# The first mixer of a transformer kernel, written anew: latents by feature tiles, roots applied at evictions and in the exponential, unnormalised probabilities

## The reference, cut to what matters

```
mod = silu(c) @ ada_w[0] + ada_b[0]            # 6 x 1024: shift1, scale1, gate1, shift2, scale2, gate2
h = rms_norm(x, norm_mix) * (1 + scale1) + shift1
proj = h @ w_in                                # 672: q_lat 384, kv_lat 256, k_rope 32
q = rms_norm(q_lat, g_qa) @ w_qb               # 16 heads of 96 (64 + 32 rotated)
kv = rms_norm(kv_lat, g_kva) @ w_kvb           # 16 heads of 64 keys + 64 values
q = [q_nope, rope(q_rope)];  k = [k_nope, rope(k_rope) for every head]
q = rms_norm(q, g_q);  k = rms_norm(k, g_k)    # over the 96 of a head
o = softmax(q k^T * 96 ** -0.5) v
x = x + gate1 * (o @ w_o)
```

## Time and profile before

| | |
|---|---|
| Median of three runs | 2139.15 us (2138.95 to 2140.81) |
| The profiled execution's own time | 2137.76 us |
| Its span in the trace | 2136.0 us |
| PE, DVE, ACT, POOL busy | 93%, 68%, 52%, 15% of the span |
| First latents matmul | 48.5 us |
| Last latents matmul ends | 67.4 us |
| First scores of the attention | 132.4 us |
| First matmul of the output product | 188.3 us |
| First matmul of the first MLP | 220.9 us |

### The profile page before, as it was taken

How to read it: one execution, slowest core, us unless ns; L and a number is a source line. 1 busy time by engine, 2 the same in 40 slices (tenths; PEclk the granted TensorE clock), 3 DMA queues, 4 the chain that set the end, 5 groups by cost and what they waited for, 6 DMA issues and landing times.

```text
span 2136.0 us, 34628 instructions
## 1 busy us (share of the span) xinstructions
PE 1994.7 (93%) x14140; PEld 1845.9 (86%) x14140; DVE 1445.9 (68%) x2553; ACT 1114.7 (52%) x1831; POOL 323.8 (15%) x338
## 2 busy tenths in 40 slices
PE   2859899899999998999889989999999999999998
PEld 1747899899988888999788889999999998888886
DVE  6697785667677756654765556889997775555554
ACT  3545553422666645543555444446767764444444
POOL 3020000000000000000000000006886970000000
PEclk7879999999999999999999999999999999999999
DMA  7534688633534433565433434554444445555553
GB/s 272 185 123 153 206 259 268 201 120 130 197 129 158 140 118 120 187 188 177 168 129 109 149 128 149 178 183 163 150 149 161 143 140 182 187 189 187 188 189 120
DMA packets 97070, 356.24 MB, mean 167 GB/s; under 512 B 10688, under 2 KB 10816, under 8 KB 96528
## 3 DMA queue, kind: packets, MB, share of 16 engines
q1 hardware_dynamic: 83824, 305.04, 42.4%
q0 software_dynamic: 12656, 48.08, 7.1%
q10 hardware_dynamic: 432, 0.90, 0.1%
HBM read 352.93 MB, written 1.05 MB: 166 GB/s over the span
## 4 chain that ended last, share of the span: by engine, by line
PE 84%; DVE 10%; ACT 4%; DMA 1%; issue 1%; SPq 0%; DVEq 0%; POOL 0%; ACTq 0%
PE psum L523 23%; PE psum L525 23%; PE psum L524 23%; PE psum L516 14%; PE psum L530 2%; DVE wl L1637 1%; DVE araw L1620 1%; DMA first<-in_ada_w 1%; ACT wh L1119 1%; ACT sqh L1107 1%; ACT work L1107 0%; DVE first L1620 0%; DVE st L1627 0%; DVE C L1617 0%; DMA araw<-in_ada_w 0%
## 5 line engine op out<-in xcount | busy, mean ns | idle before, releaser
L1637 DVE TENSOR_TENSOR wl<-raw,wh 128x1024 fp32r<-128x1024 f32 (+1 forms) x564 | 689.7, 1226 | 446.3 <-ACT wh L1119 445.7
L1119 ACT ACTIVATE wh<-raw 128x1024 fp32r<-128x1024 f32 (+1 forms) x564 | 593.1, 1053 | 473.6 <-PE psum L525 446.3
L523 PE MATMUL psum<-peer_hh,wh 128*128 128x256 f32 x1152 | 332.0, 288 | 4.2 <-DVE peer_hl L1609 4.0
L525 PE MATMUL psum<-peer_hh,wl 128*128 128x256 f32 x1152 | 326.2, 283 | 0.0
L524 PE MATMUL psum<-peer_hl,wh 128*128 128x256 f32 x1152 | 324.8, 282 | 0.0
L523 PEld LDWEIGHTS psum<-peer_hh,wh 128*128 128x128 f32 x1152 | 218.1, 189 | 5.4 <-issue 4.4
L524 PEld LDWEIGHTS psum<-peer_hl,wh 128*128 128x128 f32 x1152 | 218.7, 190 | 0.0
L525 PEld LDWEIGHTS psum<-peer_hh,wl 128*128 128x128 f32 x1152 | 216.9, 188 | 0.0
L523 PE MATMUL psum<-wh,csh 128*128 128x512 f32 x512 | 202.9, 396 | 0.0
L525 PE MATMUL psum<-wh,csl 128*128 128x512 f32 x512 | 202.7, 396 | 0.0
L524 PE MATMUL psum<-wl,csh 128*128 128x512 f32 x512 | 202.7, 396 | 0.0
(11 more groups left out here) (436 smaller groups left out, 4778.8 us busy)
## 6 DMA issues: line engine op xcount, KB each, us to landing
raw<-in_mlp_w SPq DMA_DIRECT2D x128, 512.0 KB, 4.0
raw<-in_eu SPq DMA_DIRECT2D x128, 512.0 KB, 3.3
raw<-in_ev SPq DMA_DIRECT2D x128, 512.0 KB, 3.2
araw<-in_ada_w POOLq DMA_DIRECT2D x80, 512.0 KB, 4.8
raw<-in_dil_qk SPq DMA_DIRECT2D x48, 512.0 KB, 3.4
raw<-in_dil_v SPq DMA_DIRECT2D x24, 512.0 KB, 3.9
first<-in_ada_w SPq DMA_DIRECT2D x8, 1024.0 KB, 18.1
raw<-in_w_in SPq DMA_DIRECT2D x16, 512.0 KB, 3.3
```

The lines of the kernel that those rows point to most:

```text
L523: e.matmul(o, l[0], r[0], start=start, stop=False, skip_group_check=loose)
L525: i = e.matmul(o, l[1], r[0], start=False, stop=stop, skip_group_check=loose)
L1119: e.activation(b.wh[v % NSPLIT][:, 0:cols], b.raw[v % NRAW][:, 0:cols], ACT.Copy).then_inc(S.hi, 1)
L1637: e.tensor_tensor(b.wl[v % NSPLIT][:, 0:cols], b.raw[v % NRAW][:, 0:cols], b.wh[v % NSPLIT][:, 0:cols].bitcast(F32), ALU.subtract).then_in ...
```

## The change

Only the first mixer is written anew; the work of later stages stays, with two small shifts of modulation tiles.

- **Loads and modulation.** Eight blocks of scale and shift: blocks 0, 1, 3 and 5 (`PE_ADA`) come as plain weight columns and are projected on TensorE, with the column `silu(c)` (`ccol`, a stationary of one column) against 256 columns, eight float32 matmuls each; the row is evicted by ScalarE and turned into columns by two transposes. Blocks 2, 4, 6 and 7 stay multiply-and-sums on VectorE. SyncE's queue alternates the 16 loads of 512 KB with the units of `w_in`. GpSimd no longer computes. Four of the eight `gate1` tiles are likewise projected on TensorE, in four pieces that GpSimd loads (`mod`). The angles of the rotation are computed at the very start.
- **Latents.** `w_in` is now the stationary, in eight units, one for each feature block: each adds to five banks (feature tiles) and the rotated part of the keys at once, so block k needs only its own scale and shift. The latents come out feature-major; their halves are made without the root. The root of each latent is formed from a matmul of the squares with a column of ones, and multiplied at the eviction of keys, values and queries, as ScalarE's per-token scale.
- **Heads.** Keys and values first, then queries. Squares and sums are made unit by unit. Keys are scaled in four groups on VectorE; the root of a query head isn't applied to the query but as the scale of the exponential (`aq`). ScalarE evicts all transposes.
- **Attention.** Probabilities are turned unnormalised. The values product has the turned probabilities as stationary and 64 value columns moving, token-major output, divided by the sum for two heads at once, transposed (`oT`), and split. The steps are ordered scores(i), values(i-2), turning(i-1).
- **Output product.** In rows (`rows_unit`, used elsewhere before): unit c contracts over heads 2c and 2c+1 only and adds to four banks that hold all eight output blocks. The eight units stand between steps 12 and 19, one a step. The eight residual passes and the four squares come after the last one.
- **Order.** All of it is one list, `MLA_ORDER`, that every engine follows; it has 26 ticks in place of 35.

```diff
+PE_ADA = (0, 1, 3, 5)
+PE_MODS = 1
+def mla_order():
+    out = [("tick", 0), ("kv", 0), ("tick", 0), ("kv", 1), ("tick", 0), ("kv", 2), ("tick", 0), ("kv", 3),
+           ("kroot", 0), ("q", 0), ("kscale", 0), ("kscale", 1), ("mod", 0), ("q", 1), ("kT", 0), ("kscale", 2),
+           ("kT", 2), ("q", 2), ("kT", 4), ("kT", 6), ("kscale", 3), ("qsum", 0), ("q", 3), ("mod", 1), ("qrope", 0),
+           ("kT", 8), ("tick", 0), ("kT", 10), ("q", 4), ("qT", 0), ("kT", 12), ("tick", 0), ("q", 5), ("qT", 2),
+           ("kT", 14), ("qsum", 1), ("qT", 4), ("qroot", 0), ("qT", 6)]
+    out += [("mod", 2), ("mod", 3)]
+    outer = {12: 0, 13: 1, 14: 2, 15: 3, 16: 4, 17: 5, 18: 6, 19: 7}
+    for i in range(20):
+        if i in outer:
+            out.append(("hi", outer[i]))
+        out.append(("att", i))
+        if i == 1:
+            out += [("qrope", 1), ("modrow", 0)]
+        if i in (2, 3, 4, 5):
+            out += [("qT", 4 + 2 * i)]
+        if i == 3:
+            out.append(("modcol", 0))
+        if i in outer:
+            out.append(("lo", outer[i]))
+        if i in outer:
+            out.append(("wo", outer[i]))
+        if i in range(20):
+            out.append(("tick", 0))
...
 # TensorE
+        def ada(j):
+            ps = take("ada", j)
+            for k in range(8):
+                if k % 4 == 0:
+                    pe.wait_ge(S.early[2 * j + k // 4], 16)
+                mm(ps[0:1, 0:256], m.ccol[:, k:k + 1], first[:, j, k, :], k == 0, k == 7,
+                   mark=("ada done", j) if k == 7 else None)
+            give("ada", j, sem=S.act, key=("ada", "row", j))
+        def w_in(k):
+            if k == 0:
+                for c in (3, 4, 0, 1, 2):
+                    take("lat", c)
+            j = weights("mla_w_in", k)
+            pe.wait_ge(S.dve, at["n0", "lo", k])
+            h = sp(m.hh, k)
+            for c in (3, 4, 0, 1, 2):
+                o = b.psum[:, at["bank", "lat", c], 0:256]
+                w = wsp(j, c * 128, 128)
+                mm(o, w[0], h[0], k == 0, False, loose=True)
+                mm(o, w[0], h[1], False, False, loose=True)
+                mm(o, w[1], h[0], False, k == 7, loose=True, mark=("lat", c, "done") if k == 7 else None)
+            o, w = b.psum[0:32, at["bank", "lat", 2], 256:512], wsp(j, 640, 32)
...
+                give("kvb", s, t, sem=S.act, key=("kvb", "v", s, t))
+                if (s, t) == (0, 0):
+                    for c in (3, 4):
+                        give("lat", c, sem=S.act, key=("lat", "square", c))
+                    lat_sums("kv", (3, 4), 0)
+                if (s, t) == (0, 1):
+                    k_rope()
+                if (s, t) == (1, 0):
+                    lat_sums("q", (0, 1, 2), 1)
...
+        def s3(h):
+            c = h // 2
+            if h % 2 == 0:
+                take("mla", "o", c)
+            ps = b.psum[:, at["bank", "mla", "o", c], :]
+            pe.wait_ge(S.act, at["mla", "probT", h])
+            for t in range(2):
+                z = t * 128 + (h % 2) * 64
+                for kb in range(2):
+                    a = kb * 256 + t * 128
+                    mm(ps[:, z:z + 64], m.probT[:, h % 2, a:a + 128], m.kv[:, kb, h, 64:128], kb == 0, kb == 1,
+                       mark=("mla", "pv", h) if kb == 1 and t == 1 else None)
...
+        ada(0)
+        ada(1)
+        columns(0)
+        columns(1)
+        ada(3)
+        w_in(0)
+        columns(3)
+        for k in range(1, 8):
+            w_in(k)
+            if k == 1:
+                ada(5)
+            if k == 2:
+                columns(5)
...
+            elif kind == "att":
+                if i < 16:
+                    s1(i)
+                if 0 <= i - 2 < 16:
+                    s3(i - 2)
+                if 0 <= i - 1 < 16:
+                    s2(i - 1)
+                if i >= 4 and i % 2 == 0:
+                    s4((i - 4) // 2)
+            elif kind == "wo":
+                pe.wait_ge(S.dve, at["mla", "out", i])
+                rows_unit("mla_o", "mla_w_o", i, sp(m.hh, i), i == 0, i == 7)
+        for c2 in range(4):
+            square_sums("mla_o", c2, m.ring)
...
 # ScalarE
+        def step(i):
+            if 0 <= i - 1 < 16:
+                h = i - 1
+                ac.wait_ge(S.pe, at["mla", "turned", h])
...
+                act(m.probT[:, h % 2, :], bank("mla", "t", h), ACT.Copy, mark=("mla", "probT", h))
...
+                ac.wait_ge(S.dve, at["mla", "negmax", i])
+                for t in range(2):
+                    act(m.prob[:, i % 3, t * 256:t * 256 + 256], bank("mla", "s", i)[:, t * 256:t * 256 + 256], ACT.Exp,
+                        bias=m.st[:, 1, i, t:t + 1], scale=m.aq[0][:, t, i:i + 1], accum_out=m.st[:, 2, i, t:t + 1],
+                        mark=("mla", "exp", i))
...
 # VectorE
-MOD_GROUPS = [(16, 8), (24, 16), (40, 8), (48, 16), (64, 16), (80, 8), (88, 8)]
+MOD_GROUPS = [(16 + 4 * PE_MODS, 8 - 4 * PE_MODS), (24, 16), (40, 8), (48, 16), (64, 16), (80, 8), (88, 8)]
...
+        products(2)
+        rsqrt("n0", m.ntmp[:, 256:512], m.ntmp[:, 512:768], rs)
...
+        for j in range(8):
+            if j >= 3:
+                ada(j)
+            ahead(j - AHEAD)
+            low(j)
+            if j in (1, 3, 4):
+                products({1: 4, 3: 6, 4: 7}[j])
...
 # GpSimd
+        po.wait_ge(S.early[15], 16)
+        piece(0)
+        piece(1)
+        for kind, i in MLA_ORDER:
+            if kind == "mod":
+                po.wait_ge(S.pe, at["mod", i])
+                piece(i + 2)
+            elif kind == "tick":
+                tick(1)
+        mod_until(24)
...
 # SyncE
+    for j in (2, 0, 1):
+        early(2 * j)
+        early(2 * j + 1)
+    for j in range(3):
+        weights(j)
+    for j in range(3, 8):
+        early(2 * j)
+        early(2 * j + 1)
+        weights(j)
```

More of the change, by code:

```diff
@@ L733, in mla, with columns @@
-        for s in range(4):
+        first = m.first.rearrange("p (j k n) -> p j k n", j=8, k=8)
+        def ada(j):
[6 more added lines that the diff above has]
+            give("ada", j, sem=S.act, key=("ada", "row", j))
+        def columns(j):
+            ps = take("ada col", j)
+            pe.wait_ge(S.act, at["ada", "row", j])
+            for x in range(2):
+                z = PE_ADA.index(j) * 256 + x * 128
+                turn_row(ps[:, x:x + 1], m.row3[0:1, z:z + 128],
+                         ("ada", "col", j) if x else None)
+            give("ada col", j, sem=S.dve, key=("ada", "col out", j))
@@ new lines, in k_rope, with lat_sums @@
+        def k_rope():
+            ps = take("k rope")
+            pe.wait_ge(S.act, at["k rope in"])
+            for t in range(2):
+                x = e.transpose(ps[:, t * 32:t * 32 + 32], m.krT[0:32, t * 128:t * 128 + 128], ident[0:32, 0:32])
+            x.then_inc(S.pe, 1)
+            n[0] += 1
+            at["k rope turned"] = n[0]
+            give("k rope", sem=S.act, key="k rope out")
+        def lat_sums(key, tiles, z):
+            ps = take("lat sum", key)
+            pe.wait_ge(S.act, at["lat", "square", tiles[-1]])
+            for t in range(2):
+                for c in tiles:
+                    a = c * 256 + t * 128
+                    mm(ps[:, t:t + 1], m.sqL[:, a:a + 128], ones[:, 0:1], c == tiles[0], c == tiles[-1],
+                       mark=("lat", "sum", key) if t and c == tiles[-1] else None)
+            give("lat sum", key, sem=S.act, key=(("lat", key), "ms"))
@@ new lines, in kv, with q @@
+                if (s, t) == (1, 0):
+                    lat_sums("q", (0, 1, 2), 1)
+        def q(s):
+            ps = take("qb", s)
+            j = weights("mla_w_qb", s)
+            for t in range(2):
+                for k in range(3):
+                    pe.wait_ge(S.dve, at["lat", "lo", k])
+                    mm3(ps[:, t * 256:t * 256 + 256], sp(m.latT, k, 256, t * 128, 128), wsp(j, k * 256, 256),
+                        k == 0, k == 2, unit=t == 1 and k == 2)
+            give("qb", s, sem=S.act, key=("qb", "out", s))
+            if s == 0:
+                for c in range(3):
+                    give("lat", c, sem=S.act, key=("lat", "square", c))
@@ L1283, in mla @@
[L1283 to L1292 removed]
+                r = m.ls[:, 2, 2 + t:3 + t]
+                act(m.kv[:, t, 4 * s:4 * s + 4, :], p3, ACT.Copy, scale=r, mark=("kvb", "v", s, t))
@@ L1294, in mlp @@
+        for c2 in range(4):
+            square("mla_o", c2, m.ring, ("mla_o", "out", c2))
     def mlp(layer, norm, sums):
@@ L1937, in mla @@
[L1937 to L1946 removed]
+            ts(m.kk[:, s], m.ang, float(1 / (2 * np.pi)), 0.25 * s, ALU.mult, ALU.add)
+        own()
```

693 lines of the change are left out of this document (421 added, 272 removed).

## The result

The changed kernel takes 2092.85 us (median of 4 runs, 2090.2 to 2093.95) against 2139.05 us (4 runs, 2136.97 to 2140.81): a ratio of 0.9783, 95% interval 0.9766 to 0.98, 46.2 us less. The forecast was 2095 us in a range of 2084 to 2112. The profiled execution has a span of 2091.1 us and took 2092.84.

What follows compares the result with a forecast made beforehand. The prediction took TensorE to bound the kernel almost throughout. Terms -18.1 + 2.0 - 18.9 - 10.1 + 1.4 = -43.7 on 2137.8 us gave 2094, with 1.4 for the median 2095; range 2084 to 2112.

Steps and rivals of the forecast that it cites:

- What bounds the kernel: Whole kernel: TensorE has 84% of the chain of waits; only the stretch before the first MLP matmul, 220.9 us, changes.
- Start: Up to the first latents matmul: 48.5 us falls to 30.4, a gain of 18.1.
- Latents: The latents' product: 19.0 us grows to 21, a loss of 2.
- Latents to first scores: From the latents' end to the first scores: 64.9 us falls to 46, a gain of 18.9.
- Attention and output: Attention and output product: 81.6 us falls to 71.5, a gain of 10.1, with steps 2 to 11 at 2.85 each.
- Tail: From the output product to the first MLP matmul: 6.9 us grows to 8.3, a loss of 1.4.
- The rule against it: Query units: transposes don't engage the full clock and would pull it down; some 4 us at risk by the row.
- (a): Start and latents: one-column projections run at, or leave, the lower clock, 9.4 and about 3 us, 2107; chance 20%.
- (b): Attention: the old step of 3.5 us stays, ten steps by 0.65, 2102 us; chance 13%.
- (c): Latents to first scores: roots and scalings stay in front of TensorE, 64.9 us fall only to 57, 2106; chance 10%.
- (d): From 30.4 us to the MLP: no stall left, 5, 4 and 2 us go, 2084; chance 5%.
- (e): Through the mixer: the clock stays at its lower level, 2190 us, slower; chance 2%.

Runs made afterwards that it cites:

- experiment 5: Changed kernel with `vec` loaded before the row of the condition on ScalarE's queue: 2088.41 us, ratio 0.9765.
- experiment 10: Changed kernel with five GpSimd multiplications of 128 x 1024 put back at the start, on an unused buffer: 2094.32 us, ratio 0.9784.
- experiment 6: Changed kernel with all 16 scale and shift tiles issued before the weight units that wait for a split: 2089.59 us, ratio 0.9768.
- experiment 4: Changed kernel with query roots multiplied into the queries before turning, query transposes behind the modulation pieces: 2098.3 us, ratio 0.9813.
- experiment 9: Changed kernel with VectorE's 16 attention modulation tiles loaded only in their first 256 of 1024 columns: 2092.55 us, ratio 0.9776.
- experiment 1: Changed kernel with each head's probabilities normalised on VectorE before they are turned: 2111.49 us, ratio 0.9873.
- 11: Changed kernel with two extra VectorE multiplications a head on a tile nobody reads, without TensorE waiting: 2094.51 us, ratio 0.9783.
- 12: Changed kernel with TensorE's turning of a head waiting for VectorE's reciprocal, nothing multiplied there: 2096.69 us, ratio 0.9793.
- experiment 7: Changed kernel with the tail's table load moved in front of all four squares of the residual: 2090.55 us, ratio 0.9775.
- the three orders: Changed kernel with `vec` before the condition row, tiles before waiting weight units and table load before the squares, together: 2085.49 us, ratio 0.975.
- experiment 3: Changed kernel with all 16 scale and shift tiles on VectorE and none projected on TensorE: 2093.52 us, ratio 0.9794.
- experiments 2: Changed kernel with the eight output product units after the attention's last step, not between steps 12 and 19: 2102.55 us, ratio 0.9832.

## Why the prediction was right, point by point

**What bounds the kernel.** Right: everything outside the first mixer stayed within 1.2 us, and TensorE's chain share rose.

**Start.** The gain of 18.1 was 15.7. The term that was mis-sized is the beginning of the norm's sum: "near 12.6, the same constants land first, in another order" was 15.04, because the load of `vec` stands behind one of 512 KB on its queue; experiment 5 gives back 2.4 us of start. The projections' price of 3.4 us measured 3.5, the clock stayed at 1.00, the slowed VectorE passes shrank from 9.1 to 2.8 us. But experiment 10 shows that, with the blocks on TensorE, slow passes that end 2.6 us later delay the first latents matmul by only 0.63, and the keys by 1.3 through SyncE's queue; so these passes have slack, and part of the 6.3 us that they shed was hidden. What all of them slow would have cost was not run: in experiment 10 the two `na` passes were not.

**Latents.** The loss of 2.0 was 4.0. "Uncovered this is worth 3 us" was said of SyncE's queue and left out of the sum. It was uncovered: experiment 6 gains 3.8 us at the MLP, with 1.2 in the latents and 1.9 in the hole in front of the keys.

**Latents to first scores.** 44.7 for 46. TensorE's list was 41 and was busy 41.1. The first evictions of keys came 8.2 us behind the latents, not 6.5, past the 7 that I had named as a sign of a wrong step; it did no harm, since TensorE was gapless from 67 us on and the wait was only in front (3.1 us for the latents' low half and 0.6 at 63 to 67). That sign was badly chosen. The forecast has no lower clock there, and behind that wait it was 0.50 for some 3 us. That the queries' root chain is hidden was right. Its worth, 2.5 us by the forecast, was not measured by itself: the 5.15 of experiment 4 have the scalings and the later transposes in them.

**Attention and output.** 67.0 for 71.5. The step of 2.85 was 2.68, heads 12 to 15 took 21.1 for 22, the last four 15.2 for 15.5, and the 1.5 for a last low half cost 0.9 inside these 15.2. Three terms were mis-sized: the step (1.7 us in ten), heads 12 to 15 (0.9), and the last four with the low half (1.8). The step was put down to the column's reload at 3.9 us; but VectorE's waits for it sum to 2.3 us over eight columns, experiment 9 takes back 1.4, and TensorE stands for only 0.8 us in the ten steps. The load that was said to leave VectorE's list did leave; experiments 1, 11 and 12 show that its worth, 19 us with some 5.6 of lower clock in it, lies in the place and not in the busy time, which I had not written.

**Tail.** 9.5 for 8.3. The table load that I had in it is worth 1.26 (experiment 7). The rest is the residual's first pass, which VectorE began at 166.34 behind a split of the MLP's weights; this was not tried.

**The rivals.** (a), the lower clock in the projections: not seen, 1.00 throughout. (b), the old step: no. (c), 57 us: no. (d), no stall left: not this kernel; the three orders gave 2085.49, near its 2084, but mostly by other stalls: at the start, in SyncE's queue and at the tail. (e), the clock at its lower level through the mixer: in no kernel here. It is there for 3 to 9 us behind the pause of some 3 us in front of the keys and, in some kernels, behind head 2; the longest is 17 us, in experiment 1.

**The rule against it.** From 90 to 97 us, 27 transposes stand among 36 matmuls, and the granted clock is 1.00; no stretch of the changed kernel is made of transposes for longer than 1.9 us (95.21 to 97.05). So the rule (the Trainium skill, TensorE: Matmul & The Clock Gate, Part 4: PE-mode transpose) changed nothing. Experiment 4 comes nearest to a test, with sixteen transposes alone behind a pause of 3.5 us:

```profile
102.40:105.70 3.30, 3.30 (x16) 3.09 (x17) 1.68 (x3) 1.94 (x3) 0.00 (x0) 0.51 0.45 185
105.70:107.70 2.00, 1.99 (x10) 1.44 (x8) 0.73 (x2) 1.81 (x3) 0.00 (x0) 0.96 0.00 0
```

The clock was at the lower level for all of them and went up with the scores. But matmuls behind a pause began at 0.50 too (experiment 3), so this agrees with the rule and doesn't show it.

## What to carry to other kernels

A pass is priced by the loop it closes: the same 0.62 us were nearly free beside the chain and counted in full between two TensorE instructions that wait for each other. When loads and weight units share a queue in an order written by hand, look for an issue that waits for compute, and put in front of it every load that waits for none. And read each stage against its own forecast: a total right to 0.1% hid errors of up to 4.5 us, and two of these, with the table load at the tail, were worth 7 us when undone. Before a difference of 1 to 3 us between two profiles is put down to an edit, look at the granted clock behind each pause and at kernels that leave the stretch alone.

## What the runs showed of the hardware

- An instruction of a float32 matmul (two to a matmul) with a stationary of one column and 256 moving columns takes 0.22 us, 16 of them 3.5 to 3.6, at a granted clock of 1.00; the clock stayed there through 11 us of little else (21.56 to 32.85).
- Eight instructions with 64 moving float32 columns and 128 stationary ones take 1.00 us, and their weight loads 1.08: 0.13 us an instruction, the time of its load and not the 0.05 that a quarter of the scores' 0.22 would be.
- Pauses of 8.2 us (experiment 3) and of some 3 (in front of the keys, changed kernel) were followed by the lower clock, 0.50; one of 1.5 us (experiment 6) was not. 2.49 us of work in 4 was followed by it in experiments 2 and 6 and not in the changed kernel, with the same instructions.
- Under work without a gap the lower clock lasted some 3 us in one kernel and 9 in another, again with the same instructions (changed kernel, experiment 7).
- GpSimd's tensor products made VectorE's passes with two SBUF tensors 2.4 to 4.5 times as long (1.23 to 2.91 us, 0.45 to 2.0).
- A load of `vec`, issued at 3.03 us behind a 512 KB load of the same queue, took 10.74 us to land, issued before it (at 2.13) 9.27.
